# The hidden units of a SwiGLU: a transpose on TensorE replaced by squares of 32 on VectorE and transfers between partitions

## The reference

```python
ada = (silu(c) @ w_ada + b_ada).reshape(1, 9, 1, 2048)       # sh1 sc1 gt1 sh2 sc2 gt2 sh3 sc3 gt3
h = rmsnorm(x, g_ffn1) * (1 + sc1) + sh1
x = x + 0.5 * gt1 * ((silu(h @ w1_gate) * (h @ w1_up)) @ w1_down)
h = rmsnorm(x, g_mix) * (1 + sc2) + sh2
x = x + gt2 * token_mix(h, w_in, w_out)                      # 8 attention heads, 8 retention heads
h = rmsnorm(x, g_ffn2) * (1 + sc3) + sh3
x = x + 0.5 * gt3 * ((silu(h @ w2_gate) * (h @ w2_up)) @ w2_down)
return rmsnorm(x, g_final)
```

## Time and profile before

| | |
|---|---|
| median of 3 runs | 1887.47 us (1886.23 to 1887.59) |
| profiled execution | 1886.38 us, of which the span of its engines 1884.6 us |
| busy: PE, PEld | 99%, 82% of the span |
| busy: DVE, ACT, POOL | 69%, 46%, 0% |
| TensorE clock granted, mean over the span | 0.998 |
| bytes moved | 506.62 MB, 269 GB/s |

### The profile page before, as it was taken

The page is one execution under the profiler, slowest core; times in us unless marked ns, Lnnn a source line. Parts: engine busy times, 40 slices in busy tenths (PEclk is TensorE's granted clock), DMA queues, the critical chain, the costliest instruction groups (busy, mean ns, idle before and its releaser), DMA issues.

```text
span 1884.6 us, 21327 instructions
## 1 busy us (share of the span) xinstructions
PE 1857.4 (99%) x8392; PEld 1539.4 (82%) x8392; DVE 1307.1 (69%) x1363; ACT 862.7 (46%) x987; POOL 0.2 (0%) x4
## 2 busy tenths in 40 slices
PE   6999999999999999999999999999999999999998
PEld 5888888888888888888888888888888888888886
DVE  7998888888887887776655777666655454444464
ACT  6555543334444444645544446444443334444443
POOL 0000000000000000000000000000000000000000
PEclk9999999999999999999999999999999999999999
DMA  9998889999888898686454575777765555556553
GB/s 382 416 414 329 337 331 373 371 353 353 339 344 336 341 339 289 261 322 222 134 186 151 200 246 211 268 278 278 258 212 190 191 190 192 190 189 212 190 195 138
DMA packets 117891, 506.62 MB, mean 269 GB/s; under 512 B 13728, under 2 KB 13984, under 8 KB 98464
## 3 DMA queue, kind: packets, MB, share of 16 engines
q1 hardware_dynamic: 117792, 505.27, 73.1%
HBM read 503.10 MB, written 2.12 MB: 268 GB/s over the span
## 4 chain that ended last, share of the span: by engine, by line
PE 97%; DVE 1%; DMA 1%; ACT 1%; SPq 0%; issue 0%; DVEq 0%; ACTq 0%
PE banks L1144 31%; PE banks L1146 31%; PE banks L1145 31%; PE banks L1177 1%; DMA ada_early<-w_ada_tiles 1%; PE banks L1198 0%; PE banks L1211 0%; ACT scratch L757 0%; DVE w_lo L876 0%; PE banks L1222 0%; PE banks L1250 0%; PE banks L1239 0%; PE banks L1230 0%; DVE scratch L888 0%; ACT scratch L710 0%
## 5 line engine op out<-in xcount | busy, mean ns | idle before, releaser
L876 DVE TENSOR_TENSOR w_lo<-w_raw,w_hi 128x1024 fp32r<-128x1024 f32 x652 | 794.6, 1223 | 486.0 <-ACT w_hi L659 485.2
L659 ACT CAST w_hi<-w_raw 128x1024 fp32r<-128x1024 f32 x652 | 686.5, 1054 | 958.4 <-PE banks L1146 900.7
L1144 PE MATMUL banks<-w_hi,x_split 128*128 128x512 f32 x1776 | 700.0, 394 | 3.2 <-DVE x_split L995 2.5
L1146 PE MATMUL banks<-w_hi,x_split 128*128 128x512 f32 x1776 | 692.8, 390 | 0.0
L1145 PE MATMUL banks<-w_lo,x_split 128*128 128x512 f32 x1776 | 691.9, 390 | 0.0
L1144 PEld LDWEIGHTS banks<-w_hi,x_split 128*128 128x128 f32 x1776 | 333.9, 188 | 71.8 <-issue 3.8
L1146 PEld LDWEIGHTS banks<-w_hi,x_split 128*128 128x128 f32 x1776 | 333.8, 188 | 70.4
L1145 PEld LDWEIGHTS banks<-w_lo,x_split 128*128 128x128 f32 x1776 | 334.0, 188 | 67.3
L1144 PE MATMUL banks<-w_hi,hidden 128*128 128x512 f32 x704 | 274.4, 390 | 0.0
L1146 PE MATMUL banks<-w_hi,hidden 128*128 128x512 f32 x704 | 274.0, 389 | 0.0
L1145 PE MATMUL banks<-w_lo,hidden 128*128 128x512 f32 x704 | 273.9, 389 | 0.0
(11 more groups left out here) (135 smaller groups left out, 635.1 us busy)
## 6 DMA issues: line engine op xcount, KB each, us to landing
w_raw<-w_chunks SPq DMA_DIRECT2D x656, 512.0 KB, 4.2
ada_raw<-w_ada_tiles SPq DMA_DIRECT2D x102, 1024.0 KB, 6.2
ada_early<-w_ada_tiles SPq DMA_DIRECT2D x32, 1024.0 KB, 9.3
ada_raw_low<-w_ada_tiles SPq DMA_DIRECT2D x10, 1024.0 KB, 6.2
gate_row<-gate_rows SPq DMA_DIRECT2D x3, 1024.0 KB, 5.3
residual<-x_t SPq DMA_DIRECT2D x2, 1024.0 KB, 8.2
out_t<-residual SPq DMA_DIRECT2D x4, 512.0 KB, 3.1
table<-tables SPq DMA_DIRECT2D x1, 1664.0 KB, 9.5
```

Source lines behind the costliest of these rows:

```text
L659: nc.scalar.copy(w_parts(c)[0], raw[:, c % RING, :]).then_inc(hi_ready, 1)
L876: nc.vector.tensor_tensor(lo, raw[:, c % RING, :], hi.bitcast(F32), ALU.subtract).then_inc(lo_ready, 1)
L1144: nc.tensor.matmul(o, x_hi, hi, start=(first and k == k0), stop=False, skip_group_check=True)
L1146: ins = nc.tensor.matmul(o, x_lo, hi, start=False, stop=(last and k == k0 + KC - 1), skip_group_check=True)
```

## The change

TensorE's 8 transposes of a body are gone. In their place:

- VectorE does one `transpose` per body (L936 of the new kernel), which turns each square of 32x32 in place, for a 128x1024 operand, out of the scratch buffer into the body's place in `hidden` (seen as plain float32).
- The squares are then in the wrong partitions. SyncE issues 16 transfers per body, each of 32 partitions x 256 elements (32 KB, rows of 1 KB), from `hidden` to `s3`: four behind each of the weight chunks TURN + 8 to TURN + 11.
- ScalarE rounds (`hid_hi`) from `s3` to `hidden` at TURN + 6, VectorE takes the rest (`hid_lo`) at TURN + 7. Both read or write runs of 32 elements.
- The order of hidden units within `hidden` that comes out is not the plain one; the host lays the rows of `w1_down` and `w2_down` out to fit (`turned_rows`).
- TURN is e for bodies 6 to 21; for bodies 0 to 5 it is 54, 61, 68, 75, 83, 95 (before: 54, 56, 65, 71, 85, 97).

```diff
+TURN_AT = []
+for g in GROUPS:
+    if g.kind == UP:
+        TURN_AT.append(max(g.last, OPEN_END, *[c + 7 for c in TURN_AT[-1:]]))
...
             put(e, ("product", g.n))
-            turn = e + 2 if g not in WHOLE else OPEN_END + 2 * g.n
-            put(turn, ("turn_hid", g.n))
-            put(turn + 1, ("hid_lo", g.n))
+            put(TURN_AT[g.n], ("turn_hid", g.n))
+            put(TURN_AT[g.n] + 6, ("hid_hi", g.n))
+            put(TURN_AT[g.n] + 7, ("hid_lo", g.n))
...
-        hid = nc.alloc_sbuf_tensor_at("hidden", [P, FA * NT, 2 * T], F32R, offset=low)
+        hid = nc.alloc_sbuf_tensor_at("hidden", [P, FA, 2, NT * T], F32R, offset=low)
+        hid_plain = nc.alloc_sbuf_tensor_at("hidden_plain", [P, FA, 2, NT * T], F32, offset=low)
...
+        def hid_parts(b):
+            return [hid[:, hid_at(b), i, :].rearrange("p (m q i) -> p m q i", q=4, i=32) for i in range(2)]
+
+        def moved():
+
+            return s3[:, :].rearrange("p (q m i) -> p m q i", q=4, i=32)
...
+            def move_hid(b, r):
+
+                if r == 0:
+                    sp.wait_ge(hid_turned, b + 1)
+                    if b > 0:
+                        sp.wait_ge(hid_ready, b)
+                for q in range(4):
+                    sp.dma_start(s3[32 * r:32 * r + 32, q * T:q * T + T],
+                                 hid_plain[32 * q:32 * q + 32, hid_at(b), 0, r * T:r * T + T]).then_inc(hid_moved, 16)
...
+            moves = {c + 8 + r: (b, r) for b, c in enumerate(TURN_AT) for r in range(4)}
...
                 w_chunk(c)
+                if c in moves:
+                    move_hid(*moves[c])
...
             def hid_high(b):
-                act.wait_ge(hid_turned, b + 1)
-                if b == 0:
-                    act.wait_ge(ada_step, ADA_EARLY)
-                elif b == 4:
-                    act.wait_ge(ada_step, ADA_EARLY + ADA_LOW)
-                nc.scalar.copy(hid[:, hid_tiles(b), 0:T], by_tile(4, NT)).then_inc(hid_hi, 1)
+                act.wait_ge(hid_moved, 256 * (b + 1))
+                nc.scalar.copy(hid_parts(b)[0], moved()).then_inc(hid_hi, 1)
...
+            def turn_hid(b):
+
+                dve.wait_ge(hid_f32, b + 1)
+                nc.vector.transpose(hid_plain[:, hid_at(b), 0, :].rearrange("p (r t m) -> p r t m", r=4, t=2),
+                                    hid_buf(b)[:, :].rearrange("p (t r m) -> p r t m", t=2, r=4)).then_inc(hid_turned, 1)
+
             def hid_low(b):
                 dve.wait_ge(hid_hi, b + 1)
-                tiles = hid_tiles(b)
-                nc.vector.tensor_tensor(hid[:, tiles, T:2 * T], by_tile(4, NT), hid[:, tiles, 0:T].bitcast(F32),
-                                        ALU.subtract).then_inc(hid_ready, 1)
+                hi, lo = hid_parts(b)
+                nc.vector.tensor_tensor(lo, moved(), hi.bitcast(F32), ALU.subtract).then_inc(hid_ready, 1)
...
+            def hidden(k, t):
+
+                at = (t * NT + k % NT) * P
+                return hid[:, k // NT, 0, at:at + P], hid[:, k // NT, 1, at:at + P]
...
-            def turn_hid(b):
-                pe.wait_ge(hid_f32, b + 1)
-                if b == 0:
-                    pe.wait_ge(silu_ready, 2)
-                else:
-                    pe.wait_ge(hid_ready, b)
-                h, turned = hid_buf(b), by_tile(4, NT)
-                for n in range(NT):
-                    for t in range(2):
-                        ins = nc.tensor.transpose(turned[:, n, t * P:t * P + P], h[:, t * GW + n * P:t * GW + n * P + P], ident)
-                ins.then_inc(hid_turned, 1)
...
+def turned_rows(w):
+
+    return w.reshape(BODIES, 4, NT, 32, D).transpose(0, 2, 1, 3, 4).reshape(FF, D)
```

More of the change, by code:

```diff
@@ L420, in build @@
         hid_f32 = sem("hid_f32")
+        hid_moved = sem("hid_moved")
         hid_turned = sem("hid_turned")
@@ L468, in build, with hid_at @@
         block = ctx.enter_context(nc.Block())
-        def hid_tiles(b):
+        def hid_at(b):
             n = b % BODIES
-            first = NT * (n if n < FA else n - FA)
-            return slice(first, first + NT)
+            return n if n < FA else n - FA
+        def hid_parts(b):
+            return [hid[:, hid_at(b), i, :].rearrange("p (m q i) -> p m q i", q=4, i=32) for i in range(2)]
+        def moved():
+            return s3[:, :].rearrange("p (q m i) -> p m q i", q=4, i=32)
         def hid_buf(b):
@@ L810, in ret_hi @@
                 nc.scalar.copy(y_pair(p)[0], by_tile(y_bank(p), 2)).then_inc(y_hi, 1)
-            stage = {"silu": silu, "restore": restore, "turn_hid": hid_high, "in_keep": in_keep, "squares": squares, "root": take_root,
+            stage = {"silu": silu, "restore": restore, "hid_hi": hid_high, "in_keep": in_keep, "squares": squares, "root": take_root,
                      "tail_squares": tail_squares, "warm_root": warm_root, "final": final, "mod": modulate, "turn_qk": keep_qk, "exp": exp, "turn_p": keep_p, "split_att": att_hi,
@@ L1102, in ret_lo @@
                 nc.vector.tensor_tensor(lo, by_tile(y_bank(p), 2), hi.bitcast(F32), ALU.subtract).then_inc(y_ready, 1)
-            stage = {"ada": ada_tile, "gate_col": set_gate, "mod_scale": mod_scale, "product": product, "hid_lo": hid_low,
+            stage = {"ada": ada_tile, "gate_col": set_gate, "mod_scale": mod_scale, "product": product, "turn_hid": turn_hid, "hid_lo": hid_low,
                      "residual": residual, "tail_residual": tail_residual, "partial": partial, "inverse": inverse,
@@ L1277, in turn_y @@
                 ins.then_inc(y_turned, 1)
-            stage = {"turn_hid": turn_hid, "turn_qk": turn_qk, "scores": scores, "turn_p": turn_p,
+            stage = {"turn_qk": turn_qk, "scores": scores, "turn_p": turn_p,
                      "attend": attend, "ret_scores": ret_scores, "ret_out": ret_out, "turn_y": turn_y}
@@ L1290, in operand @@
                         pe.wait_ge(hid_ready, done + i // 2 + 1)
-                    return halves(hid)
+                    return hidden
                 elif g.kind == OUT:
@@ L1324, in tail @@
                                 turn_unit(n, u)
-                        ins = product_chunk(g.first + i, halves(hid) if g.kind == DOWN else mixed, KC * i, 2 * g.side, False,
+                        ins = product_chunk(g.first + i, hidden if g.kind == DOWN else mixed, KC * i, 2 * g.side, False,
                                             i == g.count - 1, (t,))
@@ L1387, in weights_in_order @@
     flat = np.empty((CHUNKS, P, CH), np.float32)
-    ffn = [[chunks(w) for w in ws] for ws in ((w1_gate, w1_up, w1_down), (w2_gate, w2_up, w2_down))]
+    ffn = [[chunks(w) for w in ws] for ws in ((w1_gate, w1_up, turned_rows(w1_down)), (w2_gate, w2_up, turned_rows(w2_down)))]
     mix_in, mix_out = chunks(w_in), chunks(w_out)
```

## The result

The changed kernel takes 1889.90 us (median of 12 runs, 1884.56 to 1894.71), the kernel before 1886.72 on the same chip (12 runs): 1.0017 times as long, 95% interval 1.001 to 1.0025. The ratio is just under the 0.2% taken as the bound of no change (its interval reaches past it), and the time is 22 us above the forecast of 1868. The runs of the changed kernel also scatter over 10 us, where those of before lie within 2. The profiled execution took 1889.84 us (span 1888.1).

A forecast was written before the change was run, and what follows sets the result against it. TensorE, busy 99% of the span, was taken to bound the kernel: -19.8 us for the turns and +0.6 at body 10 give -19.2, so 1867.2, plus 1.1 for the median, 1868 us; range 1866 to 1876, the forecast's own 1866.5 to 1870.

The forecast's parts named there:

- The turns, 22 x 0.90: On TensorE, removing the 8 transposes of each of 22 bodies saves 0.90 us per body, 19.8 us in all.
- Transpose on VectorE, 1.22 us: One 128x1024 transpose per body on VectorE takes 1.22 us (bounds 0.84 and 2.35) and costs no time.
- their zero cost: On ScalarE and VectorE, hid_hi and hid_lo keep their size (1.01 and 1.22 us) and add zero.
- body 10: The close body: TensorE stands still about 0.6 us for hid_lo near chunk 232, more if moves come over 2 us late.
- Issue on SyncE: Four moves take 1.5 to 1.7 us to issue behind a weight chunk and fit SyncE's 2.4 us wait each time.
- Engine time, 0.09 to 0.37 us a move: On the transfer engines, a move takes 0.09 us by bytes, 0.37 if a small packet costs an average one.
- 0.4 us per chunk finds its place and 1.5 piles up: Transfer engines, first SwiGLU: moves adding 0.4 us per weight chunk fit (0.35 spare); 1.5 would pile up 4.6 us.
- Are the moves there when ScalarE comes to them?: Before hid_hi: issues end 4.8 us before ScalarE comes, landing takes 3 to 5 us, up to 1.4 us late costs nothing.
- a lead of 5.7 us: Time left between w_hi and w_lo of a chunk and TensorE's need of it, taken to cover late moves.
- (a): Moves or VectorE late in the first SwiGLU: 5.5 to 11 us given back, 1874 to 1879; chance 11%.
- (b): Moves hold the transfer queue one after another: TensorE waits from 0.59 us per move, slower above 0.64; chance 6%.
- a fixed 2 us a move one after another: Transfer queue, estimate by the skill page: 16 x 2.1 = 33 us per body against 11 available; the trace spoke against it.

The follow-up runs named there:

- e5: The changed kernel with the 16 moves of a body left out (values wrong): 1867.14 us, 0.9899 of the kernel before.
- e6: The changed kernel with 4 moves of 128x256 per body in place of 16 of 32x256 (values wrong): 1870.03 us, 0.9913 of the kernel before.
- e3: The changed kernel with its 16 moves issued by GpSimd as soon as the squares are turned: 1870.08 us, 0.9914 of the kernel before.
- e9: The changed kernel with 8 moves of 128x128 per body in place of 16 of 32x256 (values wrong): 1872.78 us, 0.9925 of the kernel before.
- e1: The changed kernel with 8 moves of 32x512 per body in place of 16 of 32x256 (values wrong): 1887.67 us, 1.0013 of the kernel before.
- e2: The changed kernel with its 16 moves cut to 32x32, an eighth of the bytes (values wrong): 1883.17 us, 0.9978 of the kernel before.
- e10: The changed kernel with squares and moves in the first SwiGLU only, TensorE's transposes in the second: 1898.13 us, 1.0055 of the kernel before.
- e4: The changed kernel with squares and moves in the second SwiGLU only, TensorE's transposes in the first: 1876.06 us, 0.9946 of the kernel before.

## Why the prediction was wrong, step by step

- **The turns, 22 x 0.90: right.** -0.89 to -0.93 each (-1.04 once), in every kernel, where no new wait hides it.
- **Transpose on VectorE, 1.22 us: right**, 1.244. `hid_hi` took 1.050 from SBUF and `hid_lo` 1.225. e5 shows that their zero cost held as long as the moves are in time, though they use up to 3 of 5.4 us of lead (chunk 72), and that body 10 costs 0.5 with moves in time (0.6 forecast). Without the moves' lateness the sum of the prediction gives 1867.2 for the profiled execution, and e5's took 1866.96.
- **Issue on SyncE, "0.38 to 0.43 us, they fit": the first step that failed.** It is 0.59 us, 0.63 from start to start. The rows used were transfers of other shapes. The check itself was the right one: the 2.4 us that SyncE waited each time had to hold four moves. At 0.63 four take 2.5, and in the first SwiGLU, with its tiles, SyncE waited only 2.2 each time (460.2 us in 206 waits between 178 and 750 us, kernel before). At a server near its limit, half as much again on a small cost was enough.
- **Engine time, 0.09 to 0.37 us a move: right as a range** (by the page (0.761 x 1888.1 - 0.731 x 1884.6) / 352 = 0.17), **too low as a price**: a move holds the queue 0.25 us, so a group 1.0. The prediction had the rule for that, 0.4 us per chunk finds its place and 1.5 piles up, and took the low end; 1.0 is over the 0.35 to spare.
- **"Are the moves there when ScalarE comes to them?": the step that decided.** Landing was about its 3 to 5 us (3.2 median over all moves; the last move of a body took 2.4 to 5.9 in the first SwiGLU). The start was not as forecast: in body 10 the last issue ended at 674.5, not 4.8 us before ScalarE's coming (673.1) but 1.4 behind it, as a group of issues with its chunk took some 0.4 us longer than TensorE's 2.72 (1.3 longer where a tile stands too), and the raw chunks behind them late too. The prediction then compared one late move with a lead of 5.7 us. But the lead is shared: late chunks, `hid_hi` waiting, and the squares and tile on VectorE all draw on it, and in bodies 0 to 4 the turns are only 7 or 8 chunks apart. In the changed kernel the time from the end of a `w_lo` to TensorE's first product of its chunk was 4.9 us at chunk 62, where the moves begin, 5.6 at chunk 70 and 0.1 at chunk 72. Of what is missing there against the kernel before (5.4), 3.0 us are missing in e5 too, so they belong to the squares and the new place of `hid_lo`, and 2.3 to the moves.
- **The clock: not priced.** 5.7 us, a quarter of the loss, are products at the lower level behind stalls. The stall of 3.95 us at 245.8 cost 6.8 with what follows it.
- **The rivals.** (a) had the place and the direction and put 5.5 to 11 us on it; it was 22. (b) set its point at 0.59 to 0.64 us per move and asked whether the transfer queue reaches it. The queue doesn't (0.25). That SyncE's 0.59 to 0.63 us fall on the same figures is chance: (b)'s 9.4 us to spare were worked out for the queue. The rival was dismissed because landings overlap, which says nothing on the engine that issues. The Trainium skill ("DMA: Bandwidth & Descriptors", Rules for kernel authors) warned against small transfers, and the direction was right; the prediction's estimate from it, a fixed 2 us a move one after another, was not seen (0.25 us of the queue a move). e6 is that rule obeyed. Another rule of that section, that spreading transfers over issuing engines brings no bandwidth and only saves issue time, fits e3, where issue time was short, as far as e3's gain is that of the free SyncE.

## What to carry to other kernels

An issue queue is an engine: add up its instructions per period, at the duration of the very shape to be issued, and treat anything near the period as a bound. A lead that covers each of several delays doesn't cover their sum; for an in-order engine ask what stands behind a wait that is itself not urgent. Where moving data takes many narrow transfers, issue them from an idle engine as soon as the data is there (e3). Transfers over all partitions are cheaper (e6, e9), but whether this rearrangement can be made of such ones was not tried.

## What the runs showed of the hardware that was not expected

- SyncE needs 0.59 us (0.507 at least) to issue a move between two sets of 32 partitions, and 0.33 us (median of 656) for a 512 KB weight chunk. GpSimd issues the same moves at 0.498 each, beside a VectorE that is over 80% busy in float32. The Trainium skill ("SBUF — State Buffer", the "DVE blocks DMA" trap) warns that GpSimd's transfers starve beside some VectorE operations, such as a float32 copy within SBUF; the longest issue in e3 was 0.633 us, so nothing of it shows here, where VectorE mostly does `tensor_tensor`, modulation tiles and transposes.
- 128 KB from SBUF to SBUF hold the queue some 1.0 us as four moves over 32 partitions and 0.39 as one over 128, with packets of the same 1 KB.
- Behind its three stalls of 3.0 to 4.2 us (changed kernel) TensorE had the lower clock level, and its products stood 0.427 us apart for 3.5 to 5.7 us. Its stalls of 0.8 to 1.6 us had nothing of the kind behind them, and neither have e3, e5 and e6, whose longest stall behind the opening is 1.5 us.
- The kernels whose TensorE stalls scatter: 10 us between the 12 runs of the changed kernel, 8.8 in e1, 7.0 in e2 and 6.6 in e10, against 1.7 in e3, 1.2 in e5 and 0.4 in e4 (4 runs each).
